# A hybrid attention and state-space layer on eight cores: another order at the borders between its stages

## The chip, the cores and the metric

The kernel runs on the 8 cores of one Trainium2 chip. Each core computes one element of the batch of 8, and no core waits for another. The time is that of one execution on the device, in microseconds (us), and it is the time of the slowest core. PE is the matrix engine (TensorE), ACT the scalar engine, DVE the vector engine, POOL is GpSimd, and SP is the engine that issues most of the transfers. Sixteen DMA engines move the data of each core.

## The reference, cut to what matters

One decoder layer over x of shape (8, 2048, 2048) in float32. One projection of x gives the inputs of two groups of heads, and their outputs go through one output projection, a residual and a LayerNorm.

```python
proj = x @ w_in                                   # (b, l, 10280)
q, k, v, f_logit, z_att, z_ssd, xbc, dt_raw = split(proj)
# forgetting attention, 8 heads x 128
F = cumsum(log_sigmoid(f_logit + b_forget), over l)
att = softmax(q k^T / sqrt(128) + F[t] - F[s], causal) v * silu(z_att)
# Mamba-2 scan, 32 heads x 64, 8 groups of B and C (128 states), chunks of 128
xs, B, C = split(silu(causal_conv4(xbc)))
dt = softplus(dt_raw + dt_bias); a_cs = cumsum(dt * A, within the chunk)
y_diag = ((C B^T) * exp(a_cs[l] - a_cs[s]), causal) (xs * dt)
state  = state * exp(a_cs[last of chunk]) + (B * exp(a_cs[last] - a_cs))^T (xs * dt)
y = y_diag + (C state_before) * exp(a_cs) + d_skip * xs
y = group_rmsnorm(y * silu(z_ssd)) * ssd_norm_w
out = layer_norm(alpha * x + concat(att, y) @ w_out)
```

So each chunk and head needs its total of `dt * A`, the last value of the running sum: its exponential decays the state, and its distance from the running sum weights the inputs of the state.

## The kernel before

The program is written as one list of instructions for each engine, in the order in which the Python code emits them. A helper (`Prog`) keeps, for each buffer, who wrote and who reads it, and puts semaphore waits in front of an instruction; each engine then works through its own list in order. So the order of emission is the order on every engine and on both issuing queues (SP's, and POOL's for transfers that also convert float32 to bf16). `inherit` lets a new buffer that takes the place of old ones wait for all who used the old ones.

1. **Start.** x arrives transposed in four quarters of 512 tokens (`xT_bf`). `start_q(q, qk0, vz_, lock)` projects a quarter: q and k of head 0 (`qk0`, 32 matmuls), and value and gate of the first pair of heads (`vz_`, four token tiles of 16 matmuls, evacuated by `vz_evac`: a copy and a tanh on ACT, then the gate `gz` on DVE). `start_fd` projects forget logits and dt, `start_qk1` q and k of head 1. Once the last `start_fd` is there, ACT takes a logarithm and DVE a scan over 2048 tokens (`Gf`), and DVE splits it into bf16 parts (`Fst`). PE transposes `Gf` (16 small transposes) and multiplies a few columns of it (`G_tok`, `g_r`). Then `load_vz(1)` fetches the value and gate weights of the second pair (2 MB) into `vz_slab`, the one buffer of its kind, which the first pair's projection still reads.
2. **Attention**, pair by pair (`hp` 0 to 3), 80 steps for each pair: a step does the scores (`S_mm`), the exponential on ACT (`E_act`, tile `P`) and the product with the values (`PV_mm`). Between them PE gets a piece of the next pair's projection (`gen_pair`). Each finished block of 512 queries is transposed by a DMA from SP (`O_tr`: `attst<-atg`) and stored (`O_st`: `mixs<-attst`). In the first 60 steps, at every odd step, a piece of `gen_dt` runs: it makes the tables of the scan (`dt_tok`, `nb_tok`, `ea_tok`, `cd_bc`, `dtde`) from dt. For the chunk totals PE transposes dt * A into `nb_tok` (16 transposes) and multiplies it with a matrix of ones in float32 (16 products, which the trace shows as 32 matmuls). The running sums go to DRAM in eight DMAs (`acs_d`).
3. **Last pair** (`hp` 3): the filler is `gen_A(0)`, projection and convolution of the first tile (4 chunks) of the scan, spread over the steps by `run_A(A_COST * (i_pair - 11) / 66)`.
4. **Scan**, 128 chunks (16 for each of 8 groups): `front(n)` (C times B on PE, `cb` and four exponentials `dec` on ACT), `front_mid(n)` (`MT` on DVE, `Xdd` and `xd` on POOL), `back_pe(n)`, `back_ew(n)` (the state `carry` on DVE, its copy `prev_bf` on ACT), with `gen_A(Q + 1)` as filler.
5. **Output projection** with LayerNorm, filled in behind the last chunks.

Between 3 and 4 stands the border that the change touches: the last `O_tr` and `O_st`, an `inherit` from all attention buffers to all buffers of the scan, then `front(0)` and `front_mid(0)`, then the loop, whose first turn starts `gen_A(1)`.

Of the kernel before, what the change touches and what calls it, by code (L numbers as in the profile page):

```python
# [7 lines left out]
F32 = mybir.dt.float32  # L8
BF16 = mybir.dt.bfloat16
# [293 lines left out]
def build_program(dbg=False, phases=3):  # L303
# [19 lines left out]
    b_acsd = Buf("acs_d")  # L323
    p = Prog(nc)
# [70 lines left out]
    cd_bc = mem.alloc([128, 16, 32], F32, "cd_bc")  # L395
# [241 lines left out]
    start_q(3, True, False, False)  # L637
# [5 lines left out]
    start_q(3, False, True, False)  # L643
# [14 lines left out]
    load_vz(1)  # L658
# [4 lines left out]
    def gen_dt():  # L663
# [8 lines left out]
        bk = nextP()  # L672
        for c in range(16):
            TR(banks[bk][:, c * 32:(c + 1) * 32], dt0[0:32, c * 128:(c + 1) * 128], ident_f[0:32, 0:32],
               [b_dt0, b_const], [bkb[bk]], signal=(c == 15))
        CPY("dve", fl(nb_tok), banks[bk][:, :], [bkb[bk]], [b_dta])
        yield
        for c in range(16):
# [4 lines left out]
            if c % 4 == 3:  # L683
# [3 lines left out]
              "acsd", reads=[b_dt0], writes=[b_acsd])  # L687
        yield
# [6 lines left out]
        bk = nextP()  # L695
        for c in range(16):
            MM(banks[bk][:, c * 32:(c + 1) * 32], ones_f[:, :], nb_tok[:, c, :], c == 0, c == 15,
               [b_dta, b_const], [bkb[bk]])
        ACT(fl(cd_bc), banks[bk][:, :], AF.Exp, [bkb[bk]], [b_ssdc])
        TT("dve", fl(dtde), banks[bk][:, :], fl(ea_tok), ALU.subtract, [bkb[bk], b_at], [b_ssdc])  # L700
# [8 lines left out]
        TT("dve", fl(nb_tok), fl(nb_tok), fl(ea_tok), ALU.subtract, [b_dta, b_at], [b_ssdc])  # L709
# [9 lines left out]
    if phases >= 1:  # L719
# [16 lines left out]
        RA = Mem(nc, o["Fst"], o["gz0"])  # L736
# [5 lines left out]
        for r_ in (RA, RB, RC, RD1, RE, RD2):  # L742
            r_.offs = offs_of
            r_.tag = "r"
# [23 lines left out]
        yn_bf.append(RA.alloc([128, 256], BF16, "yn2"))  # L768
        ysm.append(RA.alloc([128, 2, 128], BF16, "ysm2"))
        w_ex = RD2.alloc([128, 8, D], BF16, "w_ex")  # L770
        uf = [RD2.alloc([128, 256], F32, "uf%d" % i) for i in range(6)]
        cb_bf = [RA.alloc([128, 128], BF16, "cb_bf%d" % i) for i in range(2)]
        dec_bf = [RA.alloc([128, 512], BF16, "dec%d" % i) for i in range(2)]
        MT_bf = [RA.alloc([128, 512], BF16, "MT%d" % i) for i in range(2)]
        Xdd = [RA.alloc([128, 256], BF16, "Xdd%d" % i) for i in range(2)]
        xd = [RA.alloc([128, 256], F32, "xd%d" % i) for i in range(2)]
# [202 lines left out]
        def back_ew(n):  # L979
            g, c, par, cq, i2 = idx(n)  # L980
            hs4 = slice(4 * g, 4 * g + 4)
            if 0 < c < 15:
                TT("dve", v4(carry[:, :]), v4(carry[:, :]), bc4(cd_bc[:, c, hs4]), ALU.mult, [b_ssdc], [b_carry])
# [274 lines left out]
        for i, (h, g, kb) in enumerate(steps):  # L1258
# [31 lines left out]
            if hp == 3 and i_pair >= 12:  # L1290
                run_A(A_COST * (i_pair - 11) / 66)
# [10 lines left out]
            if trq and trq[0][0] <= i:  # L1302
                _, h2, g2 = trq.pop(0)
                O_tr(h2, g2)
        for _, h2, g2 in trq:
            O_tr(h2, g2)
        O_st(*stq.pop(0))
        att_bufs = ([b_F, b_Gtok, b_const] + b_q + b_k + b_gz + b_vp + b_P + b_acc + b_rv + b_atg + b_att)
        in_att[0] = False
        inherit(b_dg[1:] + b_cbst[1:] + b_normw[1:] + b_yn + b_ysm + b_w[16:24] + b_uf + b_cb + b_dec + b_MT + b_Xdd  # L1310
                + b_xd + b_t1 + b_t2 + [b_carry, b_prev] + b_normw[0:1] + [b_junk, b_nrw, b_nmr] + b_ss + b_rstd + b_st + b_mv
# [80 lines left out]
```

How the kernel before makes its waits and increments, by code:

```python
                def body(e):  # L144
                    for waits, fn, inc in self.ops[ename]:
                        for k, v in waits.items():
                            e.wait_ge(sems[k], v)
                        if fn is None:
                            continue
                        ins = fn(e)
                        if inc is not None:
                            ins.then_inc(sems[inc[0]], inc[1])
```

## Time and profile before

| | |
|---|---|
| median of 3 runs | 1933.17 us (1931.16 to 1936.24) |
| the profiled execution | 1933.39 us, the span of its slowest core 1931.8 us |
| spans of the cores | 1916.5 to 1931.8 us |
| PE busy | 1829.2 us, 95% of the span |
| DVE, ACT, POOL busy | 51%, 37%, 28% |
| chain that ended last | PE 81%, DMA 7%, DVE 5%, issue 3%, ACT 2% |

The span less PE's busy time is about 100 us; the chain of work that ended last follows the work back from the last instruction to what released it. Times in the rows below are those of the slowest core, from the start of its span.

### The profile page before, as it was taken

To read this page: it belongs to the slowest core of one execution; us is meant where nothing else is said; L and a number is where in the kernel's file an instruction comes from. 1 tells how busy PE (TensorE), PEld (TensorE's weight loads), DVE (VectorE), ACT (ScalarE), POOL (GpSimd) and SP (SyncE) were. 2 spreads that over 40 slices of the span, in tenths; PEclk is the share of its full clock that TensorE was granted. 3 is DMA by queue.
4 is the path that set the end of the run, shared out by engine and by line. 5 is a ranking of instruction groups with operands and counts; after the bars stand their busy time and mean duration, and the time that the engine had idled before them with its cause. 6 is when DMAs were issued, how large, how long until landed. Compare 5 with 4: busy or idle time off the path is not lost.

```text
span 1931.8 us, 35062 instructions; the slowest of 8 cores (1916.5 to 1931.8 us)
## 1 busy us (share of the span) xinstructions
PE 1829.2 (95%) x11798; PEld 1020.0 (53%) x11798; DVE 984.2 (51%) x2177; ACT 721.9 (37%) x1786; POOL 547.8 (28%) x730
## 2 busy tenths in 40 slices
PE   5997999999999888999999999999999997999997
PEld 2444445445445554665666656666566653444443
DVE  0032322322222344767767676767676666565565
ACT  1122443443344564555555555555555540000000
POOL 3000000000000004655656565655656550000000
PEclk9998999999999998999999999999999998999999
DMA  9908241642811521543636353633565566434431
GB/s 145 144 6 122 40 83 39 96 72 52 117 21 39 99 47 50 105 103 77 132 75 129 78 115 84 114 91 85 126 163 121 137 173 209 163 131 151 138 131 55
DMA packets 165121, 196.05 MB, mean 101 GB/s; under 512 B 96776, under 2 KB 123560, under 8 KB 158128
## 3 DMA queue, kind: packets, MB, share of 16 engines
q1 hardware_dynamic: 145552, 125.62, 24.4%
q0 software_dynamic: 19392, 68.20, 22.0%
q8 instruction: 96, 1.57, 0.3%
q14 instruction: 81, 0.66, 0.1%
HBM read 215.27 MB, written 42.22 MB: 133 GB/s over the span
## 4 chain that ended last, share of the span: by engine, by line
PE 81%; DMA 7%; DVE 5%; issue 3%; ACT 2%; POOL 1%; SPq 0%; DVEq 0%; ACTq 0%; POOLq 0%
PE bank L338 81%; DMA vz_slab<-wpack 2%; DMA w_out_bf<-wob 2%; DMA attst<-atg 2%; DMA ysm_r<-yn_r 1%; ACT P L350 1%; ACT tt L350 1%; DVE MT_r L354 1%; DVE t_r L354 0%; DVE xt L364 0%; SPq L111 0%; ACT vp L369 0%; DVE nrw_r L364 0%; DVE rstd_r L360 0%; DVE atg L364 0%
## 5 line engine op out<-in xcount | busy, mean ns | idle before, releaser
L338 PE MATMUL bank<-xT_bf,slab 128*128 128x512 bf16 x2048 | 480.0, 381 | 21.1 <-DMA xT_bf<-xT 21.1
L338 PEld LDWEIGHTS bank<-xT_bf,slab 128*128 128x128 bf16 x2048 | 197.5, 98 | 238.9 <-issue 27.3
L338 PE MATMUL bank<-vz_slab,xT_bf 128*128 128x512 bf16 x1024 | 250.5, 389 | 17.3 <-DMA vz_slab<-wpack 10.6
L338 PE MATMUL bank<-w_out_bf,mb 128*128 128x512 bf16 x1024 | 233.7, 381 | 0.0
L338 PE MATMUL bank<-xT_bf,slab_r 128*128 128x512 bf16 x1024 | 231.5, 379 | 0.0
L350 ACT ACTIVATE dec_r<-abc_r,nb_tok 128x128 bf16<-128x128 f32 x512 | 205.2, 401 | 36.3 <-ACT dec_r L350 1.1
L354 POOL TENSOR_TENSOR t_r<-t_r,xd_r 128x256 f32<-128x256 f32 x120 | 99.7, 831 | 334.6 <-DVE t_r L354 328.0
L350 ACT ACTIVATE tt<-bank 128x512 f32<-128x512 f32 (+1 forms) x256 | 138.7, 542 | 138.4 <-PE bank L338 128.5
L338 PEld LDWEIGHTS bank<-vz_slab,xT_bf 128*128 128x128 bf16 x1024 | 99.5, 100 | 126.8 <-issue 28.3
L338 PEld LDWEIGHTS bank<-w_out_bf,mb 128*128 128x128 bf16 x1024 | 100.6, 98 | 121.6 <-issue 2.5
L338 PEld LDWEIGHTS bank<-xT_bf,slab_r 128*128 128x128 bf16 x1024 | 98.9, 98 | 113.6
L354 POOL TENSOR_TENSOR abc_r<-abc_r,mask 128x512 f32<-128x512 f32 x128 | 150.6, 1177 | 13.1 <-DMA abc_r<-acs_d 12.5
L350 ACT ACTIVATE P<-bank,G_off 128x512 bf16<-128x512 f32 x192 | 125.9, 686 | 56.6 <-PE bank L338 56.6
L338 PE MATMUL bank<-vp,P 128*128 128x129 bf16 x1088 | 115.5, 221 | 22.4 <-ACT P L350 19.8
L338 PEld LDWEIGHTS bank<-vp,P 128*128 128x128 bf16 x1088 | 82.8, 98 | 98.8 <-issue 48.1
L338 PE MATMUL bank<-w_ex_r,mb 128*128 128x512 bf16 x512 | 121.1, 379 | 0.0
L338 PE MATMUL bank<-slab_r,xT_bf 128*128 128x256 bf16 x1024 | 118.0, 273 | 0.0
L350 ACT ACTIVATE sc_r<-sc_r 128x1 f32<-128x1 f32 x16 | 3.2, 203 | 305.5 <-DVE sc_r L359 305.5
L338 PE MATMUL bank<-slab,xT_bf 128*128 128x256 bf16 x1024 | 117.0, 273 | 0.0
L364 DVE SCALAR_TENSOR_TENSOR gz<-tt,bank 128x256 f32<-128x256 f32 x64 | 26.9, 421 | 167.8 <-ACT tt L350 167.6
L338 PE MATMUL bank<-qT,kT 128*128 128x512 bf16 (+1 forms) x320 | 111.1, 348 | 0.0
L370 DVE CAST kT<-bank 128x512 bf16<-128x512 f32 x32 | 22.1, 691 | 169.7 <-PE bank L338 169.7
(136 smaller groups left out, 2521.0 us busy)
## 6 DMA issues: line engine op xcount, KB each, us to landing
abc_r<-acs_d SPq DMA_DIRECT2D x128, 256.0 KB, 3.5
slab<-wpack POOLq DMA_DIRECT2D x20, 1024.0 KB, 9.9
xt<-x_tok SPq DMA_DIRECT2D x16, 1024.0 KB, 6.0
out<-xt SPq DMA_DIRECT2D x64, 256.0 KB, 2.3
wob<-w_out POOLq DMA_DIRECT2D x24, 512.0 KB, 25.2
slab_r<-wpack POOLq DMA_DIRECT2D x12, 1024.0 KB, 9.7
mb<-mixs SPq DMA_DIRECT2D x16, 768.0 KB, 5.5
xT_bf<-xT POOLq DMA_DIRECT2D x16, 512.0 KB, 45.3
```

What stands on the lines that cost most here:

```text
L338: return p.op("pe", lambda e: e.matmul(outap, lhsT, rhs, start=start, stop=stop), reads, writes, signal)
L350: return e.activation(out=outap, in_=in_, func=func, scale=scale, **kw)
L354: return p.op(eng, lambda e: e.tensor_tensor(out=outap, in0=in0, in1=in1, op=op), reads, writes)
L364: return p.op(eng, lambda e: e.scalar_tensor_tensor(out=outap, in0=in0, scalar=scalar, in1=in1, op0=op0, op1=op1), reads, writes)
L370: return p.op(eng, lambda e: e.tensor_copy(out=outap, in_=in_), reads, writes)
```

## The change

At the **start**, the last quarter's value and gate projection is emitted ahead of the transposes of `Gf`, and the q and k projection of head 0 behind them; `load_vz(1)` follows the value and gate projection directly. In **`gen_dt`**, the 16 transposes and 16 float32 products for the chunk totals are gone. The last column of each chunk's running sum is copied (`totc`), stored to DRAM (`tot_d`) and loaded back to all 128 partitions (`cd_bc`, now heads by chunks), both by DMAs from SP; `gen_dt` has one piece less. At the **border**, the first chunk's `front(0)` and `front_mid(0)` run in step 76 of the last pair, with their buffers moved to the place of q and k of a head that is done (`RA2`); `gen_A(0)` is spread over 64 instead of 66 parts of the pair; and the first 3.5 cost units of `gen_A(1)` (one projection of 16 matmuls) are emitted before the last `O_tr`.

```diff
@@ start
-    start_q(3, True, False, False)
+    start_q(3, False, True, False)
+    load_vz(1)
     gb = nextS()
     for t in range(16):
         TR(banks[gb][:, t * 8:(t + 1) * 8], Gf[0:8, ...], ident_f[0:8, 0:8], ...)
     CPY("dve", G_tok..., banks[gb][:, 0:128], [bkb[gb]], [b_Gtok])
-    start_q(3, False, True, False)
+    start_q(3, True, False, False)
...
-    load_vz(1)
     load_qk(2)
     start_qk1(3)
     load_qk(3)
@@ gen_dt
-        yield
-        bk = nextP()
-        for c in range(16):
-            TR(banks[bk][:, c * 32:(c + 1) * 32], dt0[0:32, c * 128:(c + 1) * 128], ident_f[0:32, 0:32], ...)
-        CPY("dve", fl(nb_tok), banks[bk][:, :], [bkb[bk]], [b_dta])
         yield
         for c in range(16): ... scans of dt0 ...
         p.dma("sp", [(acs_d[g]..., dt0[4 * g:4 * g + 4, :]...) for g in range(8)], "acsd", ...)
+        CPY("dve", totc[0:32, :], dt0[0:32, :].rearrange("h (c l) -> h c l", c=16)[:, :, 127], [b_dt0], [b_tot])
+        p.dma("sp", [(tot_d[:, :], totc[0:32, :])], "totd", reads=[b_tot], writes=[b_totd])
+        p.dma("sp", [(fl(cd_bc), tot_d.rearrange("h c -> (h c)").unsqueeze(0).to_broadcast([128, 512]))], "tot",
+              reads=[b_totd], writes=[b_tot])
         yield
         ... 16 transposes of dt0, CPY("dve", fl(ea_tok), ...)
         yield
-        bk = nextP()
-        for c in range(16):
-            MM(banks[bk][:, c * 32:(c + 1) * 32], ones_f[:, :], nb_tok[:, c, :], c == 0, c == 15, ...)
-        ACT(fl(cd_bc), banks[bk][:, :], AF.Exp, [bkb[bk]], [b_ssdc])
-        TT("dve", fl(dtde), banks[bk][:, :], fl(ea_tok), ALU.subtract, [bkb[bk], b_at], [b_ssdc])
+        TT("dve", dtde[:, :, :], cd_bc[:, :, :].rearrange("p h c -> p c h"), ea_tok[:, :, :], ALU.subtract,
+           [b_tot, b_at], [b_ssdc])
+        ACT(fl(cd_bc), fl(cd_bc), AF.Exp, [b_ssdc], [b_tot])
@@ buffers of the first chunk, last pair, border
+        RA2 = Mem(nc, o["qT0"], o["gz0"])          # cb_bf, dec, MT, Xdd, xd now here
...
-                run_A(A_COST * (i_pair - 11) / 66)
+                run_A(A_COST * (i_pair - 11) / 64)
+            if hp == 3 and i_pair == 76:
+                inherit(b_cb + b_dec + b_MT + b_Xdd + b_xd, [b_q[0], b_k[0]])
+                run_A(1e9)
+                front(0)
+                front_mid(0)
...
+        in_att[0] = False
+        state.update(gen=gen_A(1), spent=0.0, mark=False)
+        run_A(3.5)
         for _, h2, g2 in trq:
             O_tr(h2, g2)
         O_st(*stq.pop(0))
-        in_att[0] = False
-        inherit(... + b_cb + b_dec + b_MT + b_Xdd + b_xd + ..., att_bufs)
+        inherit(... without these five ..., att_bufs)
         p.dma("sp", [(normw[0][:, :], cp("normw", 0, 256))], "normw0", writes=[b_normw[0]])
         p.op("dve", lambda e: e.memset(cbst[1][:, :], 0.0), [], [b_cbst[1]])
-        front(0)
-        front_mid(0)
         for n in range(128 + LAG + 2):
-            if cq == 0 and n <= 124:
+            if cq == 0 and 0 < n <= 124:
                 run_A(1e9)
```

## Rows read from the trace of the kernel before

**Rows 1.** PE's waits: total us, times, longest

```profile
PE bank L338 <- DVE MT_r L354: 22.5, 6, 10.8
PE bank L338 <- DMA vz_slab<-wpack: 10.6, 2, 9.6
```

**Rows 2.** Timeline of PE, end of the start: start, us, instruction, [idle before]

```profile
120.91 7.07 PE L338 MATMUL bank<-xT_bf,slab 128*128 128x512 bf16 x32
130.08 1.55 PE L341 MATMUL bank<-ident_f,Gf 8*128 8x8 f32 x16 [2.10 <-DVE Gf L627]
131.56 16.81 PE L338 MATMUL bank<-vz_slab,xT_bf 128*128 128x512 bf16 x64
...
166.29 1.87 PE L338 MATMUL bank<-vz_slab,xT_bf 128*128 128x512 bf16 x4 [9.56 <-DMA vz_slab<-wpack]
```

**Rows 3.** Timeline of POOL, same stretch

```profile
149.10 0.53 POOL L111 DMA_DIRECT2D vz_slab<-wpack  x1 [129.58 <-PE bank L338]
```

**Rows 4.** DMA issues, 140 to 155: size, us from issue to landing

```profile
vz_slab<-wpack POOLq DMA_DIRECT2D x1, 2048.0 KB, 17.1
```

**Rows 5.** Timeline of DVE, end of the start

```profile
138.61 1.22 DVE L370 CAST Fst<-r 32x2048 bf16<-32x2048 f32 x1
```

**Rows 6.** The page's groups: busy us, mean ns, idle before

```profile
L364 DVE SCALAR_TENSOR_TENSOR gz<-tt,bank 128x256 f32<-128x256 f32 x64 | 26.9, 421 | 167.8 <-ACT tt L350 167.6
```

**Rows 7.** Window of 2 us, PE alone: busy, clock, DMA share, GB/s

```profile
172.00:174.00 2.00, 2.00 (x6) 0.50 1.07 160
```

**Rows 8.** Timeline of PE after two other waits

```profile
177.60 1.89 PE L338 MATMUL bank<-vz_slab,xT_bf 128*128 128x512 bf16 x8 [1.34 <-DVE gz L364]
...
519.60 1.86 PE L338 MATMUL bank<-vz_slab,xT_bf 128*128 128x512 bf16 x4 [3.26 <-DVE gz L364]
```

**Rows 9.** Timeline of PE around the products for the totals

```profile
205.72 1.18 PE L341 MATMUL bank<-ident_f,dt 32*128 32x32 f32 x16
...
209.69 1.89 PE L338 MATMUL bank<-vz_slab,xT_bf 128*128 128x512 bf16 x8 [1.17 <-DVE gz L364]
...
211.64 3.71 PE L338 MATMUL bank<-nb_tok,ones_f 128*128 128x32 f32 x32
...
215.67 3.46 PE L338 MATMUL bank<-vz_slab,xT_bf 128*128 128x512 bf16 x8
```

**Rows 10.** Timeline of SP's queue, first pair of heads

```profile
182.52 18.70 SPq L111 DMA_TRANSPOSE attst<-atg  x2
201.87 0.42 SPq L111 DMA_DIRECT2D mixs<-attst  x1
202.39 5.45 SPq L111 DMA_DIRECT2D acs_d<-dt  x8
```

**Rows 11.** Timeline of DVE: scans of dt, third of four groups

```profile
193.81 1.95 DVE L679 TENSOR_TENSOR_SCAN dt<-ones_f,dt 32x128 f32<-32x128 f32 x4
```

**Rows 12.** Window, PE alone: busy, clock, DMA share, GB/s

```profile
196.00:201.00 5.00, 5.00 (x32) 1.00 0.77 149
```

**Rows 13.** Landing of the 128 broadcast loads out of acs_d

```profile
DMA to landing us min/median/max: 3.0/3.5/13.8
```

**Rows 14.** The chain that ended last, border: start, us, what

```profile
724.89 3.02 DMA attst<-atg
727.97 1.96 DMA mixs<-attst
```

**Rows 15.** Timeline of PE, border to the scan

```profile
732.91 0.37 PE L338 MATMUL bank<-xs_tok_r,MT_r 128*128 128x64 bf16 x4 [10.83 <-DVE MT_r L354]
...
733.42 9.37 PE L338 MATMUL bank<-xT_bf,slab 128*128 128x512 bf16 x32
742.62 0.28 PE L338 MATMUL bank<-xs_tok_r,MT_r 128*128 128x64 bf16 x4
```

**Rows 16.** Timeline of ACT, border

```profile
730.30 1.87 ACT L350 ACTIVATE dec_r<-abc_r,nb_tok 128x128 bf16<-128x128 f32 x4
```

**Rows 17.** Timeline of DVE, border

```profile
730.23 0.48 DVE L1314 MEMSET cbst_r<- 128x512 bf16 x1 [5.48 <-DMA mixs<-attst]
```

More of the change, by code:

```diff
@@ L323, in build_program @@
     b_acsd = Buf("acs_d")
+    tot_d = nc.dram_tensor("tot_d", [32, 16], F32, kind="Internal").ap()
+    b_totd = Buf("tot_d")
+    b_tot = Buf("tot")
     p = Prog(nc)
@@ L394, in build_program @@
     ea_tok = mem.alloc([128, 16, 32], F32, "ea_tok")
-    cd_bc = mem.alloc([128, 16, 32], F32, "cd_bc")
+    cd_bc = mem.alloc([128, 32, 16], F32, "cd_bc")
+    totc = mem.alloc([128, 16], F32, "totc")
     dtde = mem.alloc([128, 16, 32], F32, "dtde")
@@ L671, in gen_dt @@
         yield
-        bk = nextP()
-        for c in range(16):
-            TR(banks[bk][:, c * 32:(c + 1) * 32], dt0[0:32, c * 128:(c + 1) * 128], ident_f[0:32, 0:32],
-               [b_dt0, b_const], [bkb[bk]], signal=(c == 15))
-        CPY("dve", fl(nb_tok), banks[bk][:, :], [bkb[bk]], [b_dta])
-        yield
         for c in range(16):
@@ L694, in gen_dt @@
         yield
-        bk = nextP()
-        for c in range(16):
-            MM(banks[bk][:, c * 32:(c + 1) * 32], ones_f[:, :], nb_tok[:, c, :], c == 0, c == 15,
-               [b_dta, b_const], [bkb[bk]])
-        ACT(fl(cd_bc), banks[bk][:, :], AF.Exp, [bkb[bk]], [b_ssdc])
-        TT("dve", fl(dtde), banks[bk][:, :], fl(ea_tok), ALU.subtract, [bkb[bk], b_at], [b_ssdc])
+        TT("dve", dtde[:, :, :], cd_bc[:, :, :].rearrange("p h c -> p c h"), ea_tok[:, :, :], ALU.subtract,
+           [b_tot, b_at], [b_ssdc])
+        ACT(fl(cd_bc), fl(cd_bc), AF.Exp, [b_ssdc], [b_tot])
         yield
@@ L708, in gen_dt @@
         yield
-        TT("dve", fl(nb_tok), fl(nb_tok), fl(ea_tok), ALU.subtract, [b_dta, b_at], [b_ssdc])
+        TT("dve", fl(nb_tok), fl(nb_tok), fl(ea_tok), ALU.subtract, [b_dta, b_at, b_tot], [b_ssdc])
         ACT(fl(ea_tok), fl(ea_tok), AF.Exp, [b_at, b_ssdc], [b_ssdc])
@@ L735, in build_program @@
         o = offs_of
-        RA = Mem(nc, o["Fst"], o["gz0"])
+        RA = Mem(nc, o["Fst"], o["qT0"])
+        RA2 = Mem(nc, o["qT0"], o["gz0"])
         RB = Mem(nc, o["gz0"], o["vz_slab"])
@@ L741, in build_program @@
         RD2 = Mem(nc, o["gz1"], mem.top)
-        for r_ in (RA, RB, RC, RD1, RE, RD2):
+        for r_ in (RA, RA2, RB, RC, RD1, RE, RD2):
             r_.offs = offs_of
@@ L767, in build_program @@
         ysm = [RD1.alloc([128, 2, 128], BF16, "ysm%d" % i) for i in range(2)]
-        yn_bf.append(RA.alloc([128, 256], BF16, "yn2"))
-        ysm.append(RA.alloc([128, 2, 128], BF16, "ysm2"))
+        yn_bf.append(RB.alloc([128, 256], BF16, "yn2"))
+        ysm.append(RB.alloc([128, 2, 128], BF16, "ysm2"))
         w_ex = RD2.alloc([128, 8, D], BF16, "w_ex")
         uf = [RD2.alloc([128, 256], F32, "uf%d" % i) for i in range(6)]
[L772 to L776, printed above, removed]
+        cb_bf = [RA2.alloc([128, 128], BF16, "cb_bf%d" % i) for i in range(2)]
+        dec_bf = [RA2.alloc([128, 512], BF16, "dec%d" % i) for i in range(2)]
+        MT_bf = [RA2.alloc([128, 512], BF16, "MT%d" % i) for i in range(2)]
+        Xdd = [RA2.alloc([128, 256], BF16, "Xdd%d" % i) for i in range(2)]
+        xd = [RA2.alloc([128, 256], F32, "xd%d" % i) for i in range(2)]
         t1 = [RA.alloc([128, 256], F32, "t1%d" % i) for i in range(2)]
@@ L982, in back_ew @@
             if 0 < c < 15:
-                TT("dve", v4(carry[:, :]), v4(carry[:, :]), bc4(cd_bc[:, c, hs4]), ALU.mult, [b_ssdc], [b_carry])
+                TT("dve", v4(carry[:, :]), v4(carry[:, :]), bc4(cd_bc[:, hs4, c]), ALU.mult, [b_ssdc], [b_carry])
             if c == 0:
@@ L1308, in build_program @@
         att_bufs = ([b_F, b_Gtok, b_const] + b_q + b_k + b_gz + b_vp + b_P + b_acc + b_rv + b_atg + b_att)
-        in_att[0] = False
-        inherit(b_dg[1:] + b_cbst[1:] + b_normw[1:] + b_yn + b_ysm + b_w[16:24] + b_uf + b_cb + b_dec + b_MT + b_Xdd
-                + b_xd + b_t1 + b_t2 + [b_carry, b_prev] + b_normw[0:1] + [b_junk, b_nrw, b_nmr] + b_ss + b_rstd + b_st + b_mv
+        inherit(b_dg[1:] + b_cbst[1:] + b_normw[1:] + b_yn + b_ysm + b_w[16:24] + b_uf + b_t1 + b_t2 + [b_carry, b_prev] + b_normw[0:1] + [b_junk, b_nrw, b_nmr] + b_ss + b_rstd + b_st + b_mv
                 + b_sc2, att_bufs)
```

## The prediction, made before the changed kernel was timed

> **What bounds the kernel now.** I read the waits of PE first, then its timeline at the places they point to, then the other engines' timelines there. PE is the bound nearly everywhere, so an edit pays only where PE stands still or runs at its lower clock. The waits name two such places that the change touches: a transfer into `vz_slab` (9.6 us at its longest) and the first `MT` of the scan (10.8 us) [rows 1]. The first is at the end of the start: PE waits 2.10 us for the scan `Gf` and later 9.56 us for the value and gate weights [rows 2]. The second is at the border to the scan [rows 15]. Times of the new order are worked out from the end of the last `start_fd`, at 120.91, up to which nothing changes [rows 2].
>
> **Value and gate first.** 32 matmuls of 512 columns take 7.07 us at the full clock, so 64 take 14.1; before they took 16.81, since they came behind the wait for `Gf` and ran partly slow [rows 2]. They now run from 120.9 to 135.0. The load was issued 0.7 us after the last of them (131.56 + 16.81 = 148.4, issue at 149.10) [rows 2, 3], and landed 17.1 us later [rows 4]. New: issue 135.8, landing 152.9. PE in the meantime has the transposes of `Gf` (1.55), 32 matmuls of head 0 (7.07), the few columns of `g_r` (under 1) and 32 of head 1 (7.07) [rows 2], which ends at about 151.6, and the first scores. So the wait for `Gf` goes (the scan is done by 130) and that for the weights shrinks to under 1 us. The first matmul of the second pair starts at 153.0 instead of 166.29: **13.3 us** (12 to 13.5).
>
> This leans on DVE. It is busy with `Fst` up to 139.8 [rows 5], and now the four gates `gz` and the copy of `G_tok` come behind that: at 0.42 each [rows 6] some 2.1 us, to 142. PE needs `G_tok` after head 0, at 143.7, and the four banks are not needed again before. The cover is thin, 1.7 us, and if it fails, the load is not late, since it doesn't wait for DVE.
>
> **Clock.** After the 9.56 us wait PE ran at 1.2 GHz: 4 matmuls took 1.87 [rows 2], the clock was still 0.50 in the window from 172 [rows 7], and 8 took 1.89 again at 177.60 [rows 8]. Of the 8.7 us from 166.3 to about 175 half comes back, less what PE would then wait for ACT: **4 us** (2 to 4.3).
>
> **Chunk totals, what goes.** 16 transposes (priced by their like, 1.18), the float32 products (3.71), and the slow stretch behind them: 8 matmuls in 3.46 instead of 1.89 [rows 9]. With the small wait that follows, **7 us** (5 to 7.4). The DVE copies are beside the path.
>
> **Chunk totals, what comes.** SP now issues eight stores of `acs_d`, the store of `tot_d`, waits for it to land, and issues the load of `cd_bc`; behind it stand `O_tr` and `O_st` of the first two blocks, whose buffers are needed again only a block or two later. DVE's subtraction waits for that load at step 17, and ACT's exponential for DVE; behind ACT's stands `E_act(18)`, so PE must wait at `PV_mm(18)`. The shift up to here is 13.3 + 4 + 1.1 (the transposes) = 18.4 us. `PV_mm(18)` followed the 8 matmuls that ended at 211.4 behind a wait of 1.17 [rows 9]: new 191.8. The scans end one piece earlier, at 195.8 before [rows 11], new 177.4; the eight stores take 5.45 to issue [rows 10], to 182.8.
> - Lower end: the store lands in about 2, as one to DRAM does [rows 14], the load in 3.0 [rows 13], with 0.4 for each issue: 188.6.
> - Upper end: SP's queue is held by the loads of weights. The first block's transposition, issued at 182.52, had landed only when its store went out at 201.87 [rows 10], 2 us after the DMA engines fell idle (a share of 0.77 of 196 to 201, so about 199.8 [rows 12]). The weights and copies queued from 149.10 thus took 50.7 us [rows 3, 12]; new they run from 135.8 to 186.5. The transposition lands at 188.6, the stores 2.5 later (an estimate from their issue), the totals at 193, the load at 197.
>
> From landing to `PV_mm(18)` go subtraction, two exponentials and signals, about 2.3 us (an estimate). So PE waits 0 at the lower end and 7.5 at the upper, with 2.5 more at the lower clock, for after a 3.26 us wait 4 matmuls took 1.86 [rows 8]. I take a landing at 194.5, nearer to the upper since before nothing of SP's landed until the weights had: 5 us and 2 for the clock, **-7 us** (0 to -10).
>
> The Trainium skill has a rule on this (DMA: Bandwidth & Descriptors, section "Queues, rings and completion order"): each DMA engine goes round the queues that have work, a packet at a time, so SP's pieces needn't wait until the weights are through. By it the landing would lie nearer to 190, and the sum at 1902; the transposition's 19.3 us in rows 10 fits both. The same page (section "Anatomy of one DMA") puts some 2 us of fixed cost on each transfer, which speaks against two in series in place of some 5 us of matmuls; the 1.96 and 3.0 us of rows 14 and 13 agree with it.
>
> **Border.** Before, PE ended the last pair at 722.1 (732.91 - 10.83 [rows 15]) and waited for `MT`, which waited for `cb` and `dec`, which inherit from the attention buffers and so waited for the last transposition (3.02) and store (1.96), landed at 729.9 [rows 14]. Now `MT` of chunk 0 is ready. Its four exponentials (1.87 [rows 16]) and `cb` stand between two exponentials of the pair, with no filler left, so the pair ends 2.0 later, at 724.1. PE goes on with 32 projection matmuls (7.07) and chunk 0 (0.5 [rows 15]) until 731.7. But DVE's clearing of `cbst` still waits for that store: before 730.23 [rows 17], new 732.2; behind it come its 0.48, `carry`, the first sum and `MT` of chunk 1, three at 0.42 [rows 6], so that PE goes on at 734.2. Before, chunk 1 began at 742.62 [rows 15]: 8.4 us. A new wait of 2.5 us lies between one that left the clock high (1.34) and one that didn't (3.26) [rows 8], which costs 0 to 3; I take 1. **7.4 us** (5 to 8.4). The 64 for 66 only moves filler by two steps and counts nothing.
>
> **Sum.** 13.3 + 4 + 7 - 7 + 7.4 = 24.7 us. The profiled execution took 1933.4, of which 1931.8 are the span of its slowest core; it stands 0.2 above the median of the runs. 1933.4 - 24.7 = **1908.7**, said as 1909.
>
> **Rivals.**
> - *The totals arrive in time* (SP's packets take turns with the weights): nothing but the clock of the start is lost; for it speaks that the stores themselves are small, against it rows 10. 1909 - 7 = 1902.
> - *The totals starve*: the worst broadcast load took 13.8 instead of 3.5 [rows 13]. At that price the landing is at 207, PE waits 17.5 and 2.5: 1909 + 13 = 1922.
> - *The start's wait comes back*: the load goes out earlier but finds the memory busier and lands as late, PE waits its 9.56 [rows 2] again. 1918.
> - *Slower than before*: the same queue, worse. Without it the gains make 31.7 us; DVE, ACT and PE all stand still until `cd_bc` is there, so from a landing at 219 on, 42 us after the scans, the kernel loses. Nothing before took that long from a free queue.
>
> **How the numbers follow.** My forecast has 0.64, the totals in time 0.20, their starving 0.08, the start's wait back 0.05, slower 0.02, no change 0.01. All ends at their best give 13.5 + 4.3 + 7.4 + 0 + 8.4 = 33.6, thus 1900; all at their worst 12 + 2 + 5 - 10 + 5 = 14, thus 1919. That range holds the first, the second and the fourth case and leaves out little more than 0.1. A change under 0.3% (6 us) can't be told from none by this measurement; so faster 0.97, same 0.01, slower 0.02.
>
> **What would show it.** The first matmul of the second pair near 153, behind a wait under 2 us, at the full clock. No float32 products; in their place a wait of PE for `P` or `gz` of 0 to 7.5 us near 192, and SP standing between `tot_d` and `cd_bc`. `MT` of chunk 0 ahead of the pair's end, a wait of 2 to 3 us before chunk 1 in place of 10.8, and everything behind shifted as one block, since the scan and the output projection are not touched. I am wrong if the wait near 192 is above 10 us, if the projection behind the start waits for weights again, or if the scan gives back what the border won.

## The result, and the profile after

Undisturbed runs of the changed kernel took 1911.69 and 1913.31 us, the kernel before beside them 1929.99 to 1936.24 (median 1932.16). The ratio is **0.9896**, with a 95% interval of 0.9866 to 0.9926: some 20 us faster, about 1912. (The two other runs, 2002.71 and 2029.2 us, had a lower clock on one half of the chip, whatever the kernel, and are left out of all comparisons here.) The forecast was 1909, with 1900 to 1919 as its range. The profiled execution took 1911.69, with a span of 1910.2 on core 1 and 1909.4 on core 3. Since the rows of before are those of core 3, I read core 3 here as well.

The waits of PE in the changed kernel (total us, times, longest), against [rows 1]:

```profile
PE bank L341 <- ACT P L353: 23.8, 33, 6.4
...
PE bank L341 <- DVE MT_r L357: 11.6, 6, 10.4
PE bank L341 <- DVE gz L367: 7.2, 3, 3.2
...
PE bank L341 <- DMA vz_slab<-wpack: 2.2, 2, 1.4
```

The wait for the weights is nearly gone (2.2 in two pieces, for 10.6) and that for `MT` has halved; its 10.4 us is another place, at the end of the scan, which was there before. New is one wait of 6.4 us for `P`. The timeline of PE at the end of the start, against [rows 2] and [rows 8], shows what the first part gave:

```profile
120.33 13.98 PE L341 MATMUL bank<-vz_slab,xT_bf 128*128 128x512 bf16 x64
134.24 1.15 PE L344 MATMUL bank<-ident_f,Gf 8*128 8x8 f32 x16
...
151.52 1.02 PE L341 MATMUL bank<-vz_slab,xT_bf 128*128 128x512 bf16 x4 [0.76 <-DMA vz_slab<-wpack]
...
158.84 1.89 PE L341 MATMUL bank<-vz_slab,xT_bf 128*128 128x512 bf16 x8 [1.34 <-DVE gz L367]
```

No wait stands ahead of the transposes of `Gf`, and the second pair's first matmul runs at 151.52 instead of 166.29, behind 0.76 us instead of 9.56. Four matmuls take 1.02 and eight 1.89, at a granted clock of 1.00. POOL's timeline has the load's issue ([rows 3]) and, 16 us later, five copies of output weights in one go:

```profile
135.04 0.64 POOL L111 DMA_DIRECT2D vz_slab<-wpack  x1 [115.41 <-PE bank L341]
...
150.96 2.57 POOL L111 DMA_DIRECT2D wob<-w_out  x5
```

The chunk totals on SP's queue, against [rows 10]:

```profile
176.27 9.24 SPq L111 DMA_DIRECT2D acs_d<-dt  x8
185.62 0.99 SPq L111 DMA_DIRECT2D tot_d<-totc  x1
189.62 0.35 SPq L111 DMA_DIRECT2D cd_bc<-tot_d  x1
```

and who stands still for them, DVE first:

```profile
193.47 1.01 DVE L357 TENSOR_TENSOR dtde<-cd_bc,ea_tok 128x512 f32<-128x512 f32 x1 [9.33 <-DMA cd_bc<-tot_d]
```

then PE, with its windows of 4 us (busy, clock, DMA share, GB/s):

```profile
196.72 0.59 PE L341 MATMUL bank<-vp,P 128*128 128x129 bf16 x4 [6.37 <-ACT P L353]
...
198.07 3.62 PE L341 MATMUL bank<-vz_slab,xT_bf 128*128 128x512 bf16 x8
```

```profile
186.00:190.00 4.00, 4.00 (x27) 1.00 0.25 70
190.00:194.00 4.00, 0.35 (x2) 0.81 0.67 131
194.00:198.00 4.00, 1.28 (x7) 0.50 0.03 6
```

PE waits 6.37 us, and the clock stays at 1.2 GHz for some 5.6 us of matmuls behind the wait (eight take 3.62 instead of 1.89).

At the border, PE's timeline, against [rows 15]:

```profile
706.75 0.33 PE L341 MATMUL bank<-vp,P 128*128 128x129 bf16 x3 [2.09 <-ACT P L353]
...
707.91 5.30 PE L341 MATMUL bank<-xT_bf,slab 128*128 128x512 bf16 x16
713.05 0.28 PE L341 MATMUL bank<-xs_tok_r,MT_r 128*128 128x64 bf16 x4
...
713.33 3.62 PE L341 MATMUL bank<-xT_bf,slab 128*128 128x512 bf16 x16
717.38 0.28 PE L341 MATMUL bank<-xs_tok_r,MT_r 128*128 128x64 bf16 x4 [0.44 <-DVE MT_r L357]
719.04 0.27 PE L341 MATMUL bank<-Xdd_r,B_tok_r 128*128 128x256 bf16 x1 [1.38 <-POOL Xdd_r L357]
```

Chunk 0 no longer waits for `MT`, and chunk 1 runs at 717.38 instead of 742.62. But the exponentials of chunk 0 make PE wait 2.09 us for a `P` at the pair's end, and 16 projection matmuls behind that take 5.30 us where 16 take 3.62 a moment later.

Where the time went is best seen from how far core 3 is ahead of before at marks that both kernels have: SP's issue of the transposition of an attention block or of the scan's `B_tok` (both counted from 0), from SP's timeline. The last column has the same for the mean of the eight cores.

| mark | before | after | ahead, us | mean of eight cores, ahead |
|---|---|---|---|---|
| attention block 3 | 264.56 | 245.99 | 18.6 | 14.7 |
| block 8 | 345.37 | 326.79 | 18.6 | 14.6 |
| block 10 | 383.89 | 369.35 | 14.5 | 14.0 |
| block 23 | 652.19 | 634.79 | 17.4 | 14.4 |
| block 31, the last | 724.89 | 711.02 | 13.9 | 10.9 |
| `B_tok` 3 | 803.30 | 779.39 | 23.9 | 21.1 |
| `B_tok` 31 | 1568.22 | 1544.88 | 23.3 | 20.3 |
| end of the span | 1931.8 | 1909.4 | 22.4 | 19.5 |

On core 3 start and totals together are worth 18.6 us; 4.1 of them are lost between blocks 8 and 10, 2.9 come back by block 23, the border brings 6.5, and the rest of the program loses 1.5. The mean of the cores has 14.7, next to nothing lost or won up to block 23, 6.7 from the border and a loss of 1.6 behind it; its 19.5 is close to the 20 of the ratio. So core 3 doesn't stand for all cores. Before, it was the latest of the eight at block 3 (264.56, the others 256.2 to 262.2), and the loss after block 8 is its own: from block 8 to 10 it takes 42.6 us, while the cores 0, 2, 5 and 7 of the changed kernel take 38.5, as six cores of the kernel before do. From block 10 to 23 it takes 265.4, before 268.3, and four cores in either kernel take 262.5 to 262.8. In both kernels it is the later core of two neighbours that loses time in the attention.

The loss of core 3 after block 8 was in nobody's sum. Timelines of POOL, SP's queue, DVE and PE of the changed kernel at that place:

```profile
316.97 0.54 POOL L111 DMA_DIRECT2D slab<-wpack  x1 [35.85 <-PE bank L341]
317.50 2.55 POOL L111 DMA_DIRECT2D wob<-w_out  x5
```

```profile
326.79 14.84 SPq L111 DMA_TRANSPOSE attst<-atg  x1
```

```profile
346.05 1.73 DVE L367 SCALAR_TENSOR_TENSOR atg<-acc,rv,gz 128x128 bf16<-128x128 f32 x4 [5.48 <-DMA attst<-atg]
```

```profile
348.25 1.02 PE L341 MATMUL bank<-vz_slab,xT_bf 128*128 128x512 bf16 x4 [2.72 <-DVE gz L367]
```

A load of weights and five copies go out together; the transposition issued 9 us later is 19.2 us (326.79 to 346.0) on its way; DVE waits for it with the next block's gating, and PE for DVE. The kernel before has the same bunch and a transposition of 16.1 us (345.37 to 361.46) there, but there DVE waited 2.37 us for it and PE not at all. This became a theory of its own, below.

### The profile page after: what moved, and what is told of

Same layout as the page of the kernel before. It is cut to its first block, busy times and chain, and to the rows that moved or that the text cites. A ratio compares the mean times of both kernels' runs of the same rounds, so it can differ in the third digit from the quotient of the medians.

```text
span 1910.2 us, 34964 instructions; the slowest of 8 cores (1896.9 to 1910.2 us)
## 1 busy us (share of the span) xinstructions
PE 1821.9 (95%) x11750; PEld 1012.8 (53%) x11750; DVE 984.6 (52%) x2177; ACT 721.7 (38%) x1786; POOL 548.3 (29%) x730
## 4 chain that ended last, share of the span: by engine, by line
PE 83%; DMA 6%; DVE 4%; issue 3%; ACT 2%; SPq 1%; POOL 1%; DVEq 0%; ACTq 0%; POOLq 0%
PE bank L341 83%; DMA vz_slab<-wpack 2%; DMA attst<-atg 1%; ACT P L353 1%; SPq L111 1%; DMA B_tok_r<-BT_r 1%; DMA ysm_r<-yn_r 1%; DMA w_out_bf<-wob 1%; ACT tt L353 1%; DVE xt L367 0%; DVE t_r L357 0%; DVE MT_r L357 0%; ACT vp L372 0%; DVE atg L367 0%; DVE nrw_r L367 0%
## 5 line engine op out<-in xcount | busy, mean ns | idle before, releaser
L341 PE MATMUL bank<-xT_bf,slab 128*128 128x512 bf16 x2048 | 481.9, 382 | 19.5 <-DMA xT_bf<-xT 19.5
L341 PE MATMUL bank<-vz_slab,xT_bf 128*128 128x512 bf16 x1024 | 245.2, 382 | 7.5 <-DVE gz L367 5.8
## 6 DMA issues: line engine op xcount, KB each, us to landing
slab_r<-wpack POOLq DMA_DIRECT2D x12, 1024.0 KB, 10.5
```

Of the source, the lines that this page charges most:

```text
L341: return p.op("pe", lambda e: e.matmul(outap, lhsT, rhs, start=start, stop=stop), reads, writes, signal)
```

## The experiments

Each was timed in five rounds against the kernel before on the same chip. The theory at the outset was the forecast's: start worth 13.3 and clock 4, totals a small loss because their landing comes too late for the step that uses them, border 7.4. The rival was that the totals are fine and that the difference to the best case is lost elsewhere.

**The three parts alone.** First, only the order at the start:

```
-    start_q(3, True, False, False)
+    start_q(3, False, True, False)
+    load_vz(1)
...
-    start_q(3, False, True, False)
+    start_q(3, True, False, False)
...
-    load_vz(1)
```

> Only the start's new order, the rest as before. Theory: the wait for the weights (9.56 us) and for the scan of the forget logits (2.1 us) go, with them 3 us of lower clock ahead and 4 behind; the first matmul of the second pair starts near 153 and the kernel is 15 to 17 us faster than before, less what a transposition that is held longer by the weights costs later (up to 4 us): ratio 0.991 to 0.994. Rival (the gain is passed on to a later wait): less than 8 us faster, ratio above 0.996.

Ratio 0.9938 (0.9924 to 0.9951), 12 us: at the lower end of what was expected, and less than the 17.3 that the forecast has for start and clock. In the timeline of its slowest core (5) the first matmul of the second pair is at 152.50, behind a wait of 1.53; the clock dips for a moment after it (eight matmuls in 2.91), which on core 3 of the whole change it doesn't.

Second, only the totals by DMAs:

```
...
-        ACT(fl(cd_bc), banks[bk][:, :], AF.Exp, [bkb[bk]], [b_ssdc])
-        TT("dve", fl(dtde), banks[bk][:, :], fl(ea_tok), ALU.subtract, [bkb[bk], b_at], [b_ssdc])
+        TT("dve", dtde[:, :, :], cd_bc[:, :, :].rearrange("p h c -> p c h"), ea_tok[:, :, :], ALU.subtract,
+           [b_tot, b_at], [b_ssdc])
+        ACT(fl(cd_bc), fl(cd_bc), AF.Exp, [b_ssdc], [b_tot])
```

> Only the chunk totals by transfers, start and border as before. Theory (the totals are held by the weights' transfers, which end near 200 here): SP's queue is free 6 us after the scans, the totals land near 209 and PE waits 2 to 3 us for them, so that of the 7 us of matmuls saved some 4 are left: ratio near 0.998. Rival (the chain is as long whatever else moves, 17 us from the end of the scans as in the changed kernel): landing near 212, PE waits 5 us and then runs at the lower clock, nothing is left: ratio 1.000 or above.

Ratio 0.9994 (0.9984 to 1.0004), nearer to the rival's 1.000 than to the theory's 0.998. PE's timeline on core 0, the slowest:

```profile
209.91 0.47 PE L341 MATMUL bank<-vp,P 128*128 128x129 bf16 x4 [2.99 <-ACT P L353]
```

This wait is the theory's, 3 us, but it is the shortest of all cores: the other seven wait 4.05 to 5.48 us, as the rival had it. What the products had cost and what the wait costs now cancel to within the measurement.

Third, only the border (the first tile's `front` and `front_mid` in step 76 of the last pair, and the buffers that allow it):

> Only the border, the rest as before. Theory: chunk 1 starts 8 to 10 us earlier against the end of the third pair, of which 2 to 3 are lost again to the four exponentials in the last pair: 6 to 8 us faster, ratio 0.996 to 0.997. Rival (the scan gives it back): ratio above 0.998.

Ratio 0.9979 (0.997 to 0.9988), 4.1 us: less than the 6 to 8 of the theory, with an interval that reaches the rival's (above 0.998). On all cores the waits at the pair's end and for `Xdd` are those of the changed kernel (2.09 for `P`, 1.38 for `Xdd`); chunk 1's `MT` is waited for 0.7 to 2.4 us (2.38 on core 0). The mean of the eight cores is 6.4 us ahead of before at `B_tok` 3 and 4.2 at the end, so the border gives what was expected and the program behind it loses 2.2 of it again; where, these runs don't show. The three parts alone add up to 12.0 + 1.2 + 4.1 = 17.3 us; together they give 20, with an interval of 14 to 26.

**The totals used later.** DVE's subtraction comes three turns of the interleaved generator later, and with it the exponential on ACT:

```
         yield
+        yield
+        yield
+        yield
         TT("dve", dtde[:, :, :], cd_bc[:, :, :].rearrange("p h c -> p c h"), ea_tok[:, :, :], ALU.subtract,
```

> The changed kernel with the use of the totals put off by three pieces of the table work, six steps. Theory: the totals land near 193, PE would ask for them near 203, the 6.4 us wait and the 3 us of lower clock behind it go: 8 to 9.5 us faster than the changed kernel, ratio to the kernel before 0.985. Rival (the subtraction only meets the end of the transfers anywhere, or another wait takes its place): within 3 us of the changed kernel, ratio 0.988 to 0.990.

Ratio **0.9855** (0.984 to 0.987). SP's queue and DVE on core 3:

```profile
189.81 0.35 SPq L111 DMA_DIRECT2D cd_bc<-tot_d  x1
```

```profile
200.27 1.01 DVE L357 TENSOR_TENSOR dtde<-cd_bc,ea_tok 128x512 f32<-128x512 f32 x1
```

The load goes out at 189.81, as late as in the changed kernel; only nobody stands still for them, and PE's wait and the low clock behind it are gone. On core 3 the marks are 8.2 us earlier at block 3 (237.80 against 245.99). So the totals' loss is one of position, as the forecast had it, and this kernel is faster than both: 1.45% against before, while the changed kernel has 1.04% (the two intervals overlap from 0.9866 to 0.987).

**Why the totals are late.** Two things could hold them: the eight stores of `acs_d` ahead of them on their own queue, and weights and copies on the DMA engines. One run starts the copies later:

```
-            if i % 10 == 0 and i < 240:
-                kb_ = i // 10
+            if i >= 50 and (i - 50) % 8 == 0 and i < 242:
+                kb_ = (i - 50) // 8
```

> The changed kernel with the 24 copies of the output weights to DRAM issued from step 50 on, every eighth step, instead of from step 0, every tenth: the five that stood behind the first weights are not there. Theory (the totals are held because SP's packets get through only as the queued weights do): the first weights are through near 170 instead of 187, the first transposition lands within 8 us instead of some 24, the totals land near 187, PE's wait near 190 falls from 6.4 to under 1.5 and the kernel is 6 to 9 us faster than the changed one: ratio to the kernel before 0.985 to 0.987. Rival (the chain is long in itself: eight stores, a store, a load): landing near 193, wait 5 to 6.4, ratio 0.989.

Ratio 0.9906 (0.987 to 0.9941), so nothing won in the time. On core 6, the slowest, the eight stores were issued in 5.06 us instead of 9.24, and PE's timeline has

```profile
195.78 0.59 PE L341 MATMUL bank<-vp,P 128*128 128x129 bf16 x4 [2.31 <-ACT P L353]
```

2.31 us where core 3 of the changed kernel had 6.37, and 1.7 at most on the other seven (the theory had under 1.5): the copies do hold the totals. The mean of the eight cores is 20.3 us ahead of before at block 3 (the changed kernel 14.7), but only 16.2 at block 23. On the way to the scan core 6 waits 3.9 us at a time for `gz` and 2.0 for `kT`, and POOL's timeline has an even larger bunch,

```profile
471.97 5.11 POOL L111 DMA_DIRECT2D wob<-w_out  x10
```

ten copies at once. The other run puts the totals ahead of the eight stores:

```
+        CPY("dve", totc[0:32, :], ...)
+        p.dma("sp", [(tot_d[:, :], totc[0:32, :])], "totd", reads=[b_tot], writes=[b_totd])
+        p.dma("sp", [(fl(cd_bc), ...)], "tot", reads=[b_totd], writes=[b_tot])
         p.dma("sp", [(acs_d[g].rearrange("c h l -> h c l"),
```

> The changed kernel with the store and the load of the totals issued ahead of the eight stores of the running sums. If SP's packets stand behind the weights until these are through (near 187): the store of the totals lands near 188, the load near 191, PE still waits 4 us. If they take turns with the weights and the eight stores were the queue: the store lands by 184, the load by 188, PE waits under 1.5 us, ratio 0.986.

Ratio 0.9889 (0.9873 to 0.9905), that of the changed kernel. SP's queue on core 7, the store's line of the DMA view (the last number is us from issue to landing), and PE:

```profile
181.50 0.33 SPq L111 DMA_DIRECT2D tot_d<-totc  x1
189.71 0.34 SPq L111 DMA_DIRECT2D cd_bc<-tot_d  x1
```

```profile
tot_d<-totc SPq DMA_DIRECT2D x1, 2.0 KB, 8.1
```

```profile
197.17 0.59 PE L341 MATMUL bank<-vp,P 128*128 128x129 bf16 x4 [5.48 <-ACT P L353]
```

The store goes out right behind the scans, but it is 8.1 us on its way, and the load can follow only at 189.71, when the DMA engines have fallen idle (a share of 0.94 at 187 to 188, 0.25 at 188 to 189, then none). Six of the eight cores show this and wait 4.5 to 5.5 us for `P`. On the slowest, core 5, it is 0.79 and on core 2 1.50, but only because their scans end at 181.4, 4 to 6 us later than on the others; core 5's load goes out no earlier:

```profile
185.33 0.33 SPq L111 DMA_DIRECT2D tot_d<-totc  x1
189.31 0.34 SPq L111 DMA_DIRECT2D cd_bc<-tot_d  x1
```

From the end of the scans to the issue of the load it is 12.4 to 14.1 us in the changed kernel, 11.0 to 12.3 on those six cores, and 7.5 to 8.3 with the copies later. So the eight stores hold the totals for 1 to 2 us, and the copies for 5 to 6: the first of the two cases of the expectation.

What holds the store on its way shows in the two queues of that core's DMA view from 173 to 187, POOL's above SP's (packets, MB, share of the engines):

```profile
q0 software_dynamic: 434, 1.58, 96.1%
q1 hardware_dynamic: 424, 0.11, 5.6%
```

The queues took turns, a packet of one for a packet of the other; in the changed kernel it was 428 to 416 from 170 to 184 on core 3. But a packet of the weights and copies had 3.6 KB on average and one of SP's 0.26. SP's queue held the transposition of block 0 then, issued at 165.09: its 128 KB make some 500 packets of that size, which is 16 to 17 us at 30 packets a us (an estimate from these two rows). The totals stand behind it in the same queue, and it is through only when the weights and copies are.

**The border.** In the changed kernel `MT` of chunk 1 waits through DVE's clearing of `cbst` for the last store of attention, because every new buffer inherits from all attention buffers. One run lets each inherit from those alone whose place it takes:

```
-        inherit(b_dg[1:] + b_cbst[1:] + ..., att_bufs)
+        inherit(b_t1 + b_t2 + ..., [b_F, b_Gtok, b_const])
+        inherit(b_dg[1:] + b_cbst[1:] + b_normw[1:] + b_yn[0:2] + b_ysm[0:2], [b_q[1], b_k[1]])
...
```

> The changed kernel with the inheritance at the border split by place: each buffer of the scan waits for those attention buffers whose bytes it takes over, not for all. Theory: DVE's clearing and the state no longer wait for the last store of attention (715.6), so the waits of PE for MT and Xdd of chunk 1 (0.4 and 1.4 us) go, and chunk 1 starts 1.5 to 2 us earlier: ratio 0.9885. Rival (chunk 1 is bound by POOL, which waits for that store anyway): no change in the trace.

Ratio 0.9898 (0.9876 to 0.9919). In its trace the wait for `MT` of chunk 1 is gone and that for `Xdd` is 0.68; from the last block to `B_tok` 2 its core 7 gains 1.6 us on core 3 of the changed kernel, and from the last block to `B_tok` 3 the mean of the cores wins 11.7 us on before, in the changed kernel 10.2. As large as expected, and too small for the timing.

Two runs fill PE's wait at the pair's end with the scan's next projection matmuls, which are let in at step 77:

```
                 front_mid(0)
+                state.update(gen=gen_A(1), spent=0.0, mark=False)
+            if hp == 3 and i_pair > 76:
+                run_A(0.88 * (i_pair - 76))
...
-        state.update(gen=gen_A(1), spent=0.0, mark=False)
         run_A(3.5)
```

> The changed kernel with the first projection of the second scan tile spread over the last three steps of the last pair instead of behind it. Theory: PE's wait of 2.1 us behind the four exponentials is filled with matmuls, the clock stays at 2.4 GHz, so that the 16 matmuls that took 5.3 us take 3.5: chunk 0 starts 3 to 4 us earlier, ratio 0.988. Rival (the border then waits for the last store in full): chunk 1 starts less than 1 us earlier.

Ratio 1.0001 (0.999 to 1.0013). The edit did more than its expectation says: the line that paces the earlier matmuls by step number still ran, and emitted the whole group of 128 matmuls within step 77. The scan's first chunks then had no filler, and its waits show the price (core 3):

```profile
PE bank L341 <- DVE MT_r L357: 29.4, 7, 10.4
```

29.4 us instead of 11.6. That says what the filler in the scan is worth, and nothing of the border. With that line ended behind step 76 (`12 <= i_pair <= 76`):

> The edit of the run before it, put right: the second projection group (its 128 matmuls) becomes available at step 77 of the last pair, is cut to 0.88 us of matmuls per step from there, and 3.5 us follow after the pair as before; the rest is left for the first chunks as in the changed kernel. Theory: in the changed kernel the last P of the pair is waited for 2.09 us with no matmul to put in its place, and the clock falls with it, so that 16 projection matmuls take 5.30 us where 3.5 is their time at full pace; filled, both go and chunk 0 starts 3 to 4 us earlier, ratio to the kernel before 0.9875 to 0.988 (changed kernel 0.9896). Rival: the matmuls put into the steps push the pair's own chain back by as much as they fill, or the first chunks miss them as filler; then 0.9896 or above.

Ratio 0.9905 (0.989 to 0.9919): the rival. PE's timeline, core 3:

```profile
710.84 0.33 PE L341 MATMUL bank<-vp,P 128*128 128x129 bf16 x3 [1.23 <-ACT P L353]
...
713.01 0.22 PE L341 MATMUL bank<-vp,P 128*128 128x129 bf16 x1
...
716.76 0.28 PE L341 MATMUL bank<-xs_tok_r,MT_r 128*128 128x64 bf16 x4 [2.66 <-DVE uT_r L373]
...
717.16 5.30 PE L341 MATMUL bank<-xT_bf,slab 128*128 128x512 bf16 x16
```

The waits at the pair's end shrink from 2.09 and 0.47 to 1.23, but chunk 0 now comes before DVE is through with the last block's gating (four products, 1.72) and `uT` (0.69). PE waits 2.66 there, and the same 16 matmuls take the same 5.30 us. From the last `P`·V of the pair to chunk 1 it is 9.5 us in both (707.85 to 717.38 before the edit, 713.01 to 722.48 with it). PE's idle time was moved, not filled.

**Together.** The later use with inheritance by place, and these two with the filled border:

> The first use of the chunk totals three turns later, and the inheritance by place in one kernel. Theory: the two act at different borders and add up: 8 us from the first (0.9855 alone) and 1.6 us from the second, 0.9845 to 0.985. Rival: the 1.6 us are lost again in the scan, ratio 0.9855 or above.

> Later use of the totals, inheritance by place and the filled border together. Theory: 8, 1.6 and 3 to 4 us add up to 13 us from the changed kernel, ratio 0.9825 to 0.984. Rival: what the borders give is taken back by waits at the scan's first chunks (their own filler is shorter by what was moved ahead) or by transposition behind weight loads; then it stands at 0.985 or above, no better than the later use alone.

Ratios 0.9861 (0.9842 to 0.9881) and 0.9861 (0.9843 to 0.9878): none is better than the later use alone, the rival both times.

**The copies spread.** The last run takes up the loss after block 8. Each copy is made to wait for the `P` of the step before its own, so that POOL no longer runs ahead and issues them in bunches; the later use is in too:

```
+                pc = Buf("pace")
+                pc.w = b_P[(i - 1) % 3].w if i else None
                 p.dma("pool", [(wob[:, kb_, :], w_v[:, kb_, :])], "wob%d" % kb_,
+                      reads=[pc],
                       writes=[b_wob[kb_]])
```

> The later use of the totals, and each of the 24 copies of output weights made to wait for the P of the step before its own, so that GpSimd no longer issues them in bunches (5 behind one another at the second pair's start, 8 at the third's, in the changed kernel's trace). Theory: these bunches lie in front of the transposition whose late landing stalls the PE in the second and third pairs (a transposition held for 14.8 us on its queue, a wait for gz of 3 us and a stretch at the low clock); spread, one copy at most is in front, the waits for gz fall from 7 us to under 2, and the slowest core ends 5 to 9 us earlier than with the later use alone: ratio to the kernel before 0.981 to 0.983 (the later use alone 0.9855). Rival: the transposition is held by the projection weights' own load (issued just ahead of each bunch) or by the neighbouring core's transfers; then the waits for gz stay and the ratio is 0.985 to 0.986.

Ratio 0.9859 (0.9838 to 0.988): the rival's time. In the attention the theory holds all the same. SP's queue on core 2, the totals and then the transposition of block 8:

```profile
176.40 5.08 SPq L111 DMA_DIRECT2D acs_d<-dt  x8
181.58 0.62 SPq L111 DMA_DIRECT2D tot_d<-totc  x1
183.91 0.35 SPq L111 DMA_DIRECT2D cd_bc<-tot_d  x1
...
317.88 1.66 SPq L111 DMA_TRANSPOSE attst<-atg  x1
```

Block 8's transposition holds the queue for 1.66 us instead of 14.84, and PE's waits for `gz` between 160 and 700 fall from 6.1 us (later use alone, core 3) to 0.4. With the later use alone the cores 0, 3, 4 and 7 wait 1.7 to 2.0 us for `gz` after block 8 and 2.5 to 3.1 near 494, and reach `B_tok` 0 at 663.6 to 665.9; the other four wait at neither place and reach it at 657.1 to 659.1. With the copies spread no core waits there, and all eight reach it at 657.4 to 661.5: the latest 4.3 us earlier, the mean 2.2. The totals, too, go from first store to load in 7.5 us instead of 13.35 (176.27 to 189.62): the copies had held them for 5.8. But the time does not follow. The slowest core of this execution is core 5, and it stands in step with its neighbour core 4 (763.69 and 763.40 at `B_tok` 3) until both issue the same loads of the next group's weights within 0.3 us. SP's queue, core 4 first, then core 5, on each the transposition of one tile of the scan and the store that follows it:

```profile
780.30 1.52 SPq L111 DMA_TRANSPOSE ysm_r<-yn_r  x1
782.62 0.32 SPq L111 DMA_DIRECT2D mixs<-ysm_r  x1
```

```profile
780.61 1.56 SPq L111 DMA_TRANSPOSE ysm_r<-yn_r  x1
793.60 0.32 SPq L111 DMA_DIRECT2D mixs<-ysm_r  x1
```

On core 4 the store follows in 2.3 us, on core 5 in 13.0; behind it on core 5 stand the loads for the next chunks and `B_tok` 4. Its window there, under that of core 4 (PE busy, clock, DMA share, GB/s):

```profile
780.00:790.00 10.00, 9.95 (x53) 1.00 1.03 194
```

```profile
780.00:790.00 10.00, 10.00 (x53) 1.00 1.26 55
```

With both cores' DMA engines full, one moved 194 GB/s and the other 55. Core 5 lost 12.4 us in this one group (119.8 us from `B_tok` 3 to 7, core 4 107.4). The other cores ended between 1887.1 and 1897.0, against 1902.5. In the two other executions the slowest core ended at 1904.5 and 1902.9; these have no profile, so what held it there is not shown.

## Why the prediction was right, point by point

**Start, 13.3: 14.2 on core 3, less on the others.** The first matmul of the second pair came 14.8 us earlier, of which 0.6 is that this core began the stretch earlier (120.33, not 120.91). The load landed 16.3 to 16.5 after its issue, the wait was under 1 us, and DVE's thin cover held: `G_tok` was copied at 141.49 and needed at 142.24. But the term was read from the core with the longest wait for the weights of all, 9.56 us; the others waited 6.2 to 9.0. In the mean of the eight cores that matmul came 11.2 us earlier.

**Clock, 4.** Held: eight matmuls behind the small wait take 1.89 instead of twice that. With the transposes gone, PE reached the step that uses the totals at 190.35 (188.46 + 1.89) instead of the 191.8 that I had worked out.

**Totals, -7: about -9.** The mechanism was right and its landing nearly exact: I took 194.5, DVE went on at 193.47. The weights were through when I had them, too: DMA share 0.96 at 184 to 186, 0.37 at 186 to 188, for 186.5 forecast. The term is off in three small pieces: PE came 1.5 earlier; from landing to PE it was 3.3 us and not 2.3, since `vp` and `tt` of the value projection stand on ACT between the two exponentials; and the low clock cost 2.8 (half of 5.6), not 2. The later use shows that this loss is all in where the step stands (0.9855 against 0.9896), and the two runs on its cause that the copies hold the totals for 5 to 6 us and the eight stores for 1 to 2. Of the two readings that I weighed, by the Trainium skill's page DMA: Bandwidth & Descriptors, section "Queues, rings and completion order", an engine goes round its queues packet by packet. The trace agrees: 434 packets of weights and copies to 424 of SP's in 14 us. But my step from there, that small pieces need not wait for the end of the weights, left out what stands ahead of them in SP's own queue, the transposition with its 500 packets or so, each of which waits for a turn. So the queues take turns, and the time still came out as by the row of before.

The pieces for start and totals, 14.2 + 4 + 7 - 9, make 16.2, and core 3's marks have 18.6. Of the 2.4 between them 0.6 is the earlier start of the stretch, and 1.2 a wait for `gz` ahead of the products [rows 9], which is gone; the rest is in small waits that I didn't follow.

**Border, 7.4: 6.5 on core 3.** Between block 23 and `B_tok` 3. The pair lost 3.5 instead of 2.0: besides the 2.09 for `P` there is a wait of 1.25 for `gz_tok` that before didn't have. The border alone has it too (1.25 on core 3), start alone and totals alone don't, so it belongs to the border; the "64 for 66" that I counted at nothing is the edit nearest to it, but that by itself wasn't tried. The low clock came at the pair's end and not at chunk 1, where I had put it: chunk 1's `MT` was waited for 0.44, not 2.5, because PE was late itself. Chunk 1 began 25.2 us earlier than before (717.38 for 742.62), that is 7.8 more than core 3 was ahead at block 23, the pair's loss counted in; 1.4 of them went to `Xdd`.

**What was missing.** "Everything behind shifted as one block" holds for the mean of the cores up to the last pair (14.7 to 14.4) and failed on core 3: 4.1 us were lost after block 8 by a transposition behind a bunch of copies, which stood there before without a wait of PE; spreading the copies removed it. It failed for all cores behind `B_tok` 3, where 1.6 us were lost. 24.7 forecast, 22.4 measured on core 3 (21.7 between the two profiled executions), 19.5 in the mean of the cores and some 20 by the ratio. On core 3 the sum is smaller by the loss after block 8, the totals, the border and the end, larger by the start and the 2.9 us that core 3 of before had lost itself; so that it comes within 2.3 us is in part luck. In the mean the terms are 14.7 for start, clock and totals (17.3 forecast) and 6.7 for the border (7.4): the waits that were to go went, and the start is the term that reading one core made too large. Of the rivals, neither the start's wait came back nor did the totals starve or arrive in time.

**What stays open.** Why one of two neighbours loses time in the attention in either kernel, and what decides which; why core 3's transposition after block 8 took 16.1 us before and 19.2 after; and where the 1.6 us behind `B_tok` 3 go.

## What to carry to other kernels

Replacing engine work by a round trip through DRAM costs nothing only if its first use stands behind the landing that the busy queues allow; read that landing from what the queues hold at that time, the transfer's own queue first, and move the use, not the transfer. Look for copies that a run-ahead queue bunches in front of small transfers that somebody waits for, and pace them. When eight cores make the time, a gain counts only if the slowest has it: here 1.6 us at the border and 4.3 us for the latest core at the scan's start didn't show in the time. And a sum read from one core is that core's sum: lay the same marks over all cores, and look at several cores before a wait is called gone.

## What the runs showed of the hardware that I had not expected

Two queues of a core take turns packet by packet (434 to 424 above), so a transposition in packets of 0.26 KB is on its way as long as the weights and copies beside it: 19.2 us with five copies bunched, 5.0 with the copies spread (317.88 to its store at 322.84, core 2).

Of two neighbouring cores one ended clearly later in the profiles that I compared. In the changed kernel the cores 0 to 3 have spans of 1903.1, 1910.2, 1898.6 and 1909.4 us: the neighbours 0 and 1 differ by 7.1 us, 2 and 3 by 10.8, the other two pairs by 10.5 and 9.3, and which one is later changes from run to run. Cores 2 and 3 drift apart where weights are loaded: 1.5 us at block 0, 6.6 at block 10, 9.4 at block 18. Twice, where neighbours issued their loads of weights at the same moment, one of them lost 12 us in one group of the scan: core 5 with the copies spread (194 against 55 GB/s, a store 13.0 us late instead of 2.3) and core 5 with the totals first (119.9 us from `B_tok` 3 to 7, all others 107.4 to 107.8), each within 0.3 us of core 4 at `B_tok` 3. With the totals first that did not make the time: cores 7 and 1 ended at 1911.1 and 1910.3 without it, core 5 at 1912.4. It isn't the whole story either: with the border alone a core lost 10 us there with its neighbour 8 us away.

What the clock did behind short waits gives no length of wait at which it falls. After 1.34 us eight matmuls took 1.89, the time at 2.4 GHz; after 2.09 and 0.47 us within 1.1 us the next 16 took 5.30 instead of 3.62; after 2.72 us (the row after block 8 above) the first four took 1.02, and the eight behind them 3.54 (granted clock 0.50 at 350 to 352). With the start alone the wait for the weights was 1.53 us on core 5 and 1.56 on core 1, and the first eight matmuls in a row behind it took 2.91 and 1.89.
